# A four-tile hybrid encoder layer on one core: the token sums of three norms and of the recurrence's heads are taken by two fp32r products with ones, the last part of a head is run inside the next head, and the first tile's first products start on undivided inputs

## The reference, cut to what matters

```python
h = _rmsnorm(x, mix_norm[l])                      # x: 2048 tokens of 1024
z = h @ w_in[l]
u, v, q, f, i, og, gates = _split_cols(z, IN_SIZES)
a = _gmlp_branch(gelu(u), gelu(v), ...)           # 4 heads, blocks of 128 tokens
b = _hgrn2_branch(q, f, i, og, ...)               # 4 heads of 128, gated recurrence
#   at its end, per head and token: o = _rmsnorm(o, norm_g) * silu(og)
y = sigmoid(gate_a) * (a @ w_br_gm[l]) + sigmoid(gate_b) * (b @ w_br_hg[l])
x = x + y @ w_out[l]
h = _rmsnorm(x, ffn_norm[l])
x = x + _conv_ffn(h, w_up[l], conv_w[l], conv_b[l], w_down[l])
return _rmsnorm(x, final_norm)

def _rmsnorm(x, g):
    return x * lax.rsqrt(jnp.mean(x * x, axis=-1, keepdims=True) + EPS) * g
```

## Time and profile before

| | |
|---|---|
| time, 3 runs | 2916.15, 2916.29 (median), 2920.58 us |
| the profiled execution | 2918.32 us, span 2916.5 us |
| mean granted TensorE clock | 0.998 of 2.4 GHz |
| PE busy | 2881.0 us (99%) |
| DVE, ACT, POOL busy | 1459.5 (50%), 710.1 (24%), 195.8 us (7%) |

### The profile page before, as it was taken

The page is one execution under the profiler, slowest core; times in us unless marked ns, Lnnn a source line. Parts: engine busy times, 40 slices in busy tenths (PEclk is TensorE's granted clock), DMA queues, the critical chain, the costliest instruction groups (busy, mean ns, idle before and its releaser), DMA issues.

```text
span 2916.5 us, 33708 instructions
## 1 busy us (share of the span) xinstructions
PE 2881.0 (99%) x13472; PEld 2397.8 (82%) x13472; DVE 1459.5 (50%) x2870; ACT 710.1 (24%) x971; POOL 195.8 (7%) x87
## 2 busy tenths in 40 slices
PE   7999999999999999999999999999999999999998
PEld 6888888888888888888888888888888888888886
DVE  2886677755266434553325634455323563355521
ACT  3332244433122112221112211222111211122210
POOL 3323410014000000000000000000000000000000
PEclk9999999999999999999999999999999999999999
DMA  7657888889743465556564445555656345555554
GB/s 269 236 184 236 316 284 293 288 304 322 253 159 132 163 224 188 190 200 229 204 217 144 145 172 218 188 193 197 231 204 215 132 143 196 208 188 197 193 204 171
DMA packets 121979, 614.61 MB, mean 211 GB/s; under 512 B 13536, under 2 KB 13792, under 8 KB 74080
## 3 DMA queue, kind: packets, MB, share of 16 engines
q1 hardware_dynamic: 121824, 612.46, 59.8%
HBM read 474.00 MB, written 138.41 MB: 210 GB/s over the span
## 4 chain that ended last, share of the span: by engine, by line
PE 93%; DMA 2%; DVE 2%; issue 1%; POOL 1%; ACT 0%; SPq 0%; POOLq 0%; DVEq 0%; ACTq 0%
PE bank L889 26%; PE bank L890 26%; PE bank L894 26%; PE bank L950 3%; PE bank L937 2%; PE bank L938 2%; PE bank L939 2%; DMA w_split<-w_both 1%; POOL w_both L384 1%; DMA raw<-w_units 1%; PE bank L903 1%; PE bank L900 1%; PE bank L901 0%; PE bank L920 0%; PE bank L991 0%
## 5 line engine op out<-in xcount | busy, mean ns | idle before, releaser
L889 PE MATMUL bank<-h_hi,w_both 128*128 128x512 f32 x2400 | 945.5, 394 | 0.0
L890 PE MATMUL bank<-h_lo,w_both 128*128 128x512 f32 x2400 | 934.3, 389 | 0.0
L894 PE MATMUL bank<-h_hi,w_both 128*128 128x512 f32 x2400 | 593.5, 389 | 0.0
L890 PEld LDWEIGHTS bank<-h_lo,w_both 128*128 128x128 f32 x2400 | 450.7, 188 | 96.9 <-issue 4.8
L889 PEld LDWEIGHTS bank<-h_hi,w_both 128*128 128x128 f32 x2400 | 450.7, 188 | 96.9 <-issue 4.8
L894 PEld LDWEIGHTS bank<-h_hi,w_both 128*128 128x128 f32 x2400 | 450.5, 188 | 93.6
L811 DVE TENSOR_TENSOR z<-bank,rms_inv 128x512 f32<-128x512 f32 x176 | 121.8, 692 | 355.3 <-PE bank L894 347.7
L889 PE MATMUL bank<-g_hi,w_both 128*128 128x512 f32 x704 | 275.4, 391 | 0.0
L890 PE MATMUL bank<-g_lo,w_both 128*128 128x512 f32 x704 | 273.9, 389 | 0.0
L824 DVE SCALAR_TENSOR_TENSOR conv<-z,params,conv 128x512 f32<-128x512 f32 x352 | 263.7, 750 | 6.2
L384 POOL TENSOR_TENSOR w_both<-raw,w_both 128x1024 fp32r<-128x1024 f32 x80 | 194.7, 2434 | 531.4 <-ACT w_both L398 504.5
(11 more groups left out here) (187 smaller groups left out, 3055.4 us busy)
## 6 DMA issues: line engine op xcount, KB each, us to landing
w_both<-w_split SPq DMA_DIRECT2D x372, 1024.0 KB, 4.8
w_split<-w_both SPq DMA_DIRECT2D x248, 512.0 KB, 5.5
raw<-w_units SPq DMA_DIRECT2D x124, 512.0 KB, 5.3
x_in<-x_t SPq DMA_DIRECT2D x32, 256.0 KB, 5.5
res<-x_t SPq DMA_DIRECT2D x32, 256.0 KB, 5.1
out<-res SPq DMA_DIRECT2D x32, 256.0 KB, 6.8
masks<-masks_in SPq DMA_DIRECT2D x1, 1152.0 KB, 9.7
gm_w<-gm_wt SPq DMA_DIRECT2D x1, 256.0 KB, 6.9
```

The costliest lines, as they stand in the source:

```text
L889: pe.matmul(dst, w_hi[slot][:, off + k, :], rhs_hi(k), start=first and k == 0, stop=False)
L890: pe.matmul(dst, w_hi[slot][:, off + k, :], rhs_lo(k), start=False, stop=False)
L894: mm = pe.matmul(dst, w_lo[slot][:, off + k, :], rhs_hi(k), start=False, stop=last and k == n - 1)
```

## The change

It has six parts.

1. At the FFN's norm, the next tile's norm and the final norm (except the very first and very last), `token_sums`, root, reciprocal, diagonal and `norm_spread` go. The sums are split into hi and lo (one ScalarE copy, one VectorE subtraction), two fp32r products with ones of 128 columns (`sums_spread`) put the sum on every partition, and root and reciprocal are taken on the full 128 x 512.
2. A head's squared output is split as well (`sq_hi`, `sq_lo`), and `o_sum` becomes two fp32r products.
3. `o_sum` of head h-1 stands on TensorE after unit f of head h (for the last head after the first gate unit), its root on ScalarE after head h's `sig_nf`, and the tail on VectorE (`recurrence_out(h - 1)`) between head h's q and qp.
4. `level(1)` and the diagonal product become one product of 192 columns (`q_both`).
5. In the first tile the eight token units multiply undivided inputs (`hx_hi`, `hx_lo` from x times the norm's weight), and the rows are scaled at the eviction. The loads are reordered so that chunk 0 and unit 0 come first; the first norm's sums, its spread and the gMLP constant's product move in between the units.
6. The factor of a norm on every partition is read from SBUF (`rms_first`, `rms_next`, `rms_done`) instead of from PSUM bank 7 or 5.

The core of the diff:

```diff
+        load_x(0, 0)
+        load_raw(0)
+        load_x(0, 1)
+        load_x(0, 2)
+        load_x(0, 3)
+        load_raw(1)
+        for c in range(4, KD):
...
+        first_hi(0)
+        first_weights(0)
+        first_hi(1)
+        for c in range(2):
+            pre_square(0, c)
+        first_weights(1)
...
+                    if u == 0:
+                        for c in range(4, 6):
+                            pre_square(0, c)
+                        for c in range(6, 8):
+                            first_hi(c)
+                    if u == 1:
+                        for c in range(6, 8):
+                            pre_square(0, c)
+                    if u == 2:
+                        norm_rms(0)
+                    if u == 3:
+                        act.wait_ge(*norm_pe.at("spread", 0))
+                        act.activation(rms_first[:, :], bank[7][:, :], ACT.Copy).then_inc(rms_spread, 1)
+                        act.wait_ge(*norm_dve.at("inv", 0))
...
+            def o_rms(it):
+                act.wait_ge(*o_pe.at("sum", it))
+                act.wait_ge(*o_dve.at("lo", it))
+                act.activation(head_o[:, :], bank[5][:, :], ACT.Sqrt, bias=eps[:, 0:1],
+                               scale=1.0 / P).then_inc(*o_act.did("rms"))
...
                 act.activation(sig_f[:, :], bank[0][:, :], ACT.Sigmoid).then_inc(*head_act.did("sig_f"))
+                if h:
+                    act.wait_ge(*o_pe.at("sum", it - 1))
                 act.activation(sig_nf[:, :], bank[0][:, :], ACT.Sigmoid, scale=-1.0).then_inc(evac[0], 1)
+                if h:
+                    o_rms(it - 1)
                 unit_behind(t, U_HEAD + 1, u)
                 act.activation(sig_q[:, :], bank[1][:, :], ACT.Sigmoid).then_inc(*head_act.did("sig_q"))
...
+                act.activation(head_o[:, :], bank[4][:, :], ACT.Square).then_inc(*o_act.did("sq"))
+                act.wait_ge(*o_act.at("sq", it))
+                act.activation(sq_hi[:, :], head_o[:, :], ACT.Copy).then_inc(*o_act.did("hi"))
 
             for p in range(KD // 2):
                 unit_behind(t, U_MIX + 4 * p)
+                if p == 0:
+                    o_rms(t * NH + NH - 1)
                 act.activation(gate_a[NH + p], bank[0][:, :], ACT.Sigmoid).then_inc(evac[0], 1)
...
+            def recurrence_out(h):
+
+                it = t * NH + h
+
+                def then(name):
+                    dve.wait_ge(*o_dve.at(name, it))
+
+                dve.wait_ge(*o_act.at("rms", it))
+                dve.reciprocal(head_o[:, :], head_o[:, :]).then_inc(*o_dve.did("inv"))
+                then("inv")
+                dve.tensor_tensor(head_o[:, :], head_o[:, :], bank[4][:, :], ALU.mult).then_inc(*o_dve.did("unit"))
+                then("unit")
+                dve.scalar_tensor_tensor(out=head_o[:, :], in0=head_o[:, :], scalar=par_col(C_HGN), in1=og_act[:, :],
+                                         op0=ALU.mult, op1=ALU.mult).then_inc(*o_dve.did("b"))
+                then("b")
+                dve.tensor_scalar(b_hi[:, h, :], head_o[:, :], 1.0, None, ALU.mult).then_inc(*o_dve.did("b_hi"))
+                then("b_hi")
+                dve.tensor_tensor(b_lo[:, h, :], head_o[:, :], b_hi[:, h, :].bitcast(F32),
+                                  ALU.subtract).then_inc(*o_dve.did("b_lo"))
+
...
+                dve.tensor_tensor(q0, blocks(sig_q[:, :], P), blocks(bank[1][:, :], P), ALU.mult).then_inc(evac[1], 1)
                 then("floor")
+                if h:
+                    recurrence_out(h - 1)
                 dve.wait_ge(evac[1], used + 1)
-                dve.tensor_tensor(qp[:, :], q0[:, :], total[1][:, :], ALU.mult).then_inc(*head_dve.did("qp1"))
+                dve.tensor_tensor(blocks(qp[:, :], P), q0, blocks(total[1][:, :], P),
+                                  ALU.mult).then_inc(*head_dve.did("qp1"))
...
+            dve.wait_ge(*ffn_act.at("sum_hi", t))
+            dve.tensor_tensor(r_lo[:, :], sum_r[:, :], r_hi[:, :].bitcast(F32), ALU.subtract).then_inc(*ffn_dve.did("sum_lo"))
             dve.wait_ge(*ffn_act.at("rms", t))
-            inverse(tok_f, diag_f, ffn_dve, t)
+            dve.reciprocal(rms_inv[:, :], rms_inv[:, :]).then_inc(*ffn_dve.did("inv"))
...
+        def sums_spread(dst, hi, lo, made, pe_steps):
+
+            pe.wait_ge(*made)
+            pe.matmul(dst[:, :], ones_r[:, :], hi[:, :], start=True, stop=False)
+            pe.matmul(dst[:, :], ones_r[:, :], lo[:, :], start=False, stop=True).then_inc(*pe_steps.did("spread"))
...
+        def for_first_tokens(n, dst, is_i):
+
+            slot, n4 = slot_of(0, U_TOK + n), n % 4
+            weights_here(pe, 0, U_TOK + n, False)
+            for lower in range(2):
+                if lower:
+                    weights_here(pe, 0, U_TOK + n, True)
+                for k in range(2 * n4, 2 * n4 + 2):
+                    cols = slice((k % 2) * NC, (k % 2 + 1) * NC)
+                    if is_i and not lower:
+                        pe.wait_ge(hx_hi_made, k + 1)
+                        pe.wait_ge(hx_lo_made, k + 1)
+                    for c in range(NC):
+                        tok = slice(c * P, (c + 1) * P)
+                        if lower:
+                            mm = pe.matmul(dst[c][:, :], hx_hi[:, k, tok], w_lo[slot][:, cols, :], start=False, stop=k == KD - 1)
+                            continue
+                        if is_i and k == 0 and c >= 2:
+                            pe.wait_ge(evac[I_BANKS[c]], B_TOK)
+                        if n == 4 and k == 0 and c == NC - 1:
+                            pe.wait_ge(rms_spread, 1)
+                        pe.matmul(dst[c][:, :], hx_hi[:, k, tok], w_hi[slot][:, cols, :], start=k == 0, stop=False)
+                        pe.matmul(dst[c][:, :], hx_lo[:, k, tok], w_hi[slot][:, cols, :], start=False, stop=False)
+            mm.then_inc(unit_done, 1)
...
+                if t == 0:
+                    for_first_tokens(n, [bank[b] for b in I_BANKS], True)
+                    if n == 1:
+                        pe.wait_ge(pro_pool, 3)
+                        for h in range(NH):
+                            mm = pe.matmul(bank[6][:, h * P:(h + 1) * P], lnb_row[:, h * P:(h + 1) * P], gm_w[:, h, :],
+                                           start=True, stop=True)
+                        mm.then_inc(pro_pe, 1)
+                    if n == 2:
+                        pe.wait_ge(*pre_dve.at("sum", KD - 1))
+                        token_sums(bank[5], sum_n).then_inc(first_ssq, 1)
+                    if n == 3:
+                        norm_spread(bank[7], diag_n, first_diag, norm_pe)
+                    continue
...
+            def o_sum(it):
+
+                pe.wait_ge(*o_dve.at("lo", it))
+                pe.matmul(bank[5][:, :], ones_r[:, :], sq_hi[:, :], start=True, stop=False)
+                pe.matmul(bank[5][:, :], ones_r[:, :], sq_lo[:, :], start=False, stop=True).then_inc(*o_pe.did("sum"))
...
                 from_h(t, U_HEAD, u, 0, used)
+                if h:
+                    o_sum(it - 1)
...
-                level(1).then_inc(*head_pe.did("s1"))
                 for c in range(NC):
-                    cols = slice(c * P, (c + 1) * P)
-                    mm = pe.matmul(bank[4][:, cols], kp[1][:, cols], q0[:, cols], start=True, stop=True)
-                mm.then_inc(*head_pe.did("diag"))
+                    mm = pe.matmul(first[:, c // 2, c % 2, :], kp[1][:, c * P:(c + 1) * P], q_both[:, c, :],
+                                   start=True, stop=True)
+                mm.then_inc(*head_pe.did("s1"))
...
-                pe.wait_ge(*head_act.at("o_sq", it))
-                pe.matmul(bank[5][:, :], ones[:, :], head_o[:, :], start=True,
-                          stop=True).then_inc(*head_pe.did("o_sum"))
 
             def gates(u, uses):
                 for j in range(2):
                     from_h(t, U_MIX + j, u, j, uses)
+                    if u == 0 and j == 0:
+                        o_sum(t * NH + NH - 1)
...
-            pe.wait_ge(*head_dve.at("b_lo", t * NH + (NH - 1)))
+            pe.wait_ge(*o_dve.at("b_lo", t * NH + (NH - 1)))
-            token_sums(bank[4], sum_r).then_inc(*ffn_pe.did("ssq"))
+            sums_spread(bank[5], r_hi, r_lo, ffn_dve.at("sum_lo", t), ffn_pe)
```

More of the change, by code:

```diff
@@ L136, in build @@
     ones = place("ones", [P, P])
+    ones_r = place("ones_r", [P, P], F32R)
     eps = place("eps", [P, 1])
@@ L176, in build @@
     head_o = place("head_o", [P, TT], F32, late + BLK)
+    rms_first = place("rms_first", [P, TT], F32, late + BLK)
     k_tok = place("k_tok", [P, TT], F32, late + 2 * BLK)
@@ L221, in build @@
     tok_act = Steps(sem("tok_act"), ["i0", "i1"] + [f"v{c}" for c in range(NC)])
-    head_act = Steps(sem("head_act"), ["i_head", "sig_f", "sig_q", "sig_og", "k_tok", "o_sq", "o_rms"])
-    head_pe = Steps(sem("head_pe"), ["s1", "diag", "k_tok", "s64_32", "s16_8", "s4_2", "update", "o", "mix", "o_sum"])
```

(29 more changed lines are left out.)

249 lines of the change are left out of this document (153 added, 96 removed).

## The result

The changed kernel takes 2953.59 us (median of 4 runs, 2952.51 to 2956.87) against 2917.08 for the kernel before (4 runs): ratio 1.0123, 95% interval 1.0107 to 1.0138. It is slower, as I said, but by 36.5 us and not by 19: the time lies outside of my range.

What follows compares the result with a forecast made beforehand. TensorE's own work was taken to bound the kernel. The terms -13.3 - 8.6 - 1.9 + 22.8 + 7.0 + 12.8 = +18.8 on the profiled 2918.3 gave 2937.1, stated as 2935 us against the median; range 2908 to 2948.

Steps and rivals of the forecast that it cites:

- What bounds the kernel: Whole kernel: TensorE's own work; time can be lost only as a new TensorE wait.
- Norm sums: FFN, next-tile and final norms: shorter sums and spread on TensorE save 13.3 us, with `r_lo` 0.9 late in the first tile.
- The start: First loads and token units: TensorE begins near 7.7 us, later waits for `sum_n`; -8.6 us, from -14 to -5.
- Later tiles' heads: Heads of tiles 2 to 4: a 0.95 us wait for t128 gives back nine heads' savings; -1.9 us together.
- First tile's heads: Three heads of the first tile: TensorE waits 8.05 us for t128, `b` held by a GpSimd burst; +22.8 us.
- The mixer: Behind each tile's first gate unit: TensorE waits for the last head's tail, 3.0 us in three tiles, 5.75 in the first; +12.8.
- The lost clock: Behind three first-tile waits of 8 us: TensorE's clock halves for 4.6 us of work; +7.0, bounds 0 and 7.
- the covered tail: Rival, first tile's heads and mixer: VectorE finishes t128 by `flip`, so the change is faster, -14 us, 2902; chance 0.14.
- Cancelling: Rival, whole kernel: no clock lost, start at its best, mixer at 2.4, so savings and waits cancel at +4.6 us; chance 0.10.
- The start did not fail: Denies the rival that chunk loads arrive no earlier, turning the start's -8.6 into about +2, 2946 us; chance 0.06.

Runs made afterwards that it cites:

- run 9: The kernel of run 5 with 14 products that nobody reads ahead of the first tile's wait for `sum_n`: 2886.89 us, ratio 0.9898.
- run 3: The changed kernel with the late tail on VectorE ahead of q instead of behind it: 2938.90 us, ratio 1.0068.
- run 4: The changed kernel with only each tile's last head having its `o_sum` (fp32), root and tail at its own end again: 2934.37 us, ratio 1.0059.
- run 1: The changed kernel with parts 2 and 3 taken back, all tails in place again: 2892.75 us, ratio 0.9914.
- run 7: The changed kernel with 64 small fp32 products ahead of the wait for t128 in heads 1 to 3 of the first tile: 2953.18 us, ratio 1.0127.
- run 8: The kernel before with parts 2 and 3 alone: 2975.61 us, ratio 1.0202.
- run 5: The changed kernel with the late tail only in heads 0 to 2 of tiles 2 to 4, ahead of q, other tails in place: 2888.26 us, ratio 0.9907.

## Why the prediction was right in direction and wrong in size

- **What bounds the kernel**: right. TensorE's own work and its waits hold the whole span, and the stage table closes to 0.5 us.
- **Norm sums, -13.3**: the mechanism was right, the trace has -15.1. 1.1 of the difference is a wait for a load of 1.3 us that is 0.2 now, which is no merit of the products. `r_lo` is late by 0.8 in the first tile (I took 0.9).
- **The start, -8.6**: the trace has -7.9. The first product at 6.81 (I said 7.7), the wait for `sum_n` 3.3 (4). Behind that wait too the clock was low, for 3.4 us, for which I had no term; run 9 shows it.
- **Later tiles' heads, -1.9**: -2.4. The saving of parts 2 and 4 is given back as a wait ahead of `flip`, as I worked out; run 3 showed that the tail's place behind q is what gives it back.
- **First tile's heads, +22.8**: +19.6. The wait is 7.18 where I had 8.05, and `b` is held by the burst as I had it. It ends 0.55 after the burst (132.68 against 132.13), though, and not with it; I had misread qp in the same way, which ended at 130.84 and its burst at 130.29. The rule of the Trainium skill that I weighed (page "SBUF — State Buffer", section "Who interferes with whom") agrees with the trace: `b` 1.81 in place of 0.75, `unit` unchanged at 0.69. The same section also counts copies in the two-port modes among what is held, and the copies of 2.47 and 2.37 us (0.29 elsewhere) fit that.
- **The mixer, +12.8**: +12.2, run 4 confirms it.
- **The lost clock, "+7.0 ... The bounds are 0 and 7"**: this is the term that failed. The mechanism was right, the size was 31.7. Three things were wrong in it. I priced the low stretch at 4.6 us, which I had read at the start, where dense units follow; behind `flip` follow small fp32 passes, and it lasts 10 to 20 us. I counted it for three heads alone; the mixer's four waits, 13.5 us together, lost 1.7 each, and the wait of head 0 lost 4.85 in the profiled execution. And I set the upper bound equal to my estimate: the row from which I priced it was of another kind of work, and so was no bound. With 31.7 in its place my sum for the profiled execution is 2961.8 against the measured 2956.87: 4.9 above, the 5.4 by which the other terms were too high less the 0.5 that the table leaves open. That these errors went the other way made the miss smaller; this was luck.
- **The rivals**: the covered tail (2902) is refuted by the waits of 7.2. In run 1 the tails are covered and it takes 2892.75. Cancelling needed no lost clock. The start did not fail.

## What to carry to other kernels

When an edit adds a wait to TensorE, price the wait and then, apart from it, the clock behind it, and look at what TensorE does next: here the low level lasted 3.4 to 10.2 us where dense products followed, and 10.2 to 20.5 us where small fp32 passes did. Work that leaves TensorE's path still has to be put where the other engine is idle: the same tail cost 60 us behind q and in the last head (waits and clock together), and gained 4 ahead of q in the tiles where VectorE had waited there. A wait that can't be removed can be filled with products that nobody reads; here that gave back 25.9 of 36.5 us.

## What I had not expected of the hardware

- Small fp32 passes kept TensorE's clock at the 2.4 GHz level for 14 us (run 7, 127 passes at 1.00). The same kind of passes behind a wait ran at the 1.2 GHz level from first to last, 10.6 us of them in the second head of the changed kernel (149.13 to 159.78).
- In the waits of 5 us and more that came after the first products, the clock fell before the wait was over. Behind waits of 2.7 to 3.3 us it fell in all but one case (the third tile's mixer in run 3), up to some 2 us after the wait had ended, and in run 8 once behind a wait of 1.8 us for a load. Behind the wait of 1.2 us in head 0 of the first tile it fell in the profiled execution of the changed kernel, and not in the profiled executions of the seven other kernels that leave that head's wait as it is. So the same program probably loses some 5 us there or doesn't; no trace of its other executions is there to show it.
- The low level behind one and the same wait differs in length: behind the wait of 3.1 to 3.3 us for `sum_n` it lasted 3.4 us in the changed kernel and 6.8 in the kernel of run 5, with no difference in the code there.
- A burst of GpSimd holds one-input copies of VectorE too (0.29 to 2.47 us), not the reciprocal: one that began inside a burst, with 0.43 us of it left, took 3.35 us as elsewhere.

```profile
295.67 2.39 POOL L413 TENSOR_TENSOR w_both<-raw,w_both 128x1024 fp32r<-128x1024 f32 x1 [6.70 <-ACT w_both L427]
...
297.63 3.35 DVE L777 RECIPROCAL head_o<-head_o 128x512 f32<-128x512 f32 x1 [5.28 <-ACT head_o L534]
```
